# Opening of a two-layer hybrid encoder kernel: x sent ahead of the modulation weights, the last quarter of the modulation formed by ScalarE and GpSimd, and the first five weight tiles split by halves

## What is computed

```python
c_act = jax.nn.silu(c)
for l in range(DEPTH):
    mod = c_act @ w_ada[l] + b_ada[l]                    # w_ada[l]: 1024 x 3072
    shift, scale, gate = jnp.split(mod, 3, axis=-1)
    h = _rmsnorm(x, norm_w) * (1.0 + scale[:, None]) + shift[:, None]
    proj = h @ w_in                                      # 1024 x 8464 columns, split among the mixers
```

## Time and profile before

| | |
|---|---|
| median of three runs | 1181.65 us |
| the profiled execution: time | 1183.2 us |
| the profiled execution: span | 1181.5 us |
| TensorE busy | 1144.8 us, 97% of the span |
| VectorE, ScalarE, GpSimd busy | 629.0, 514.1 and 518.0 us |
| mean granted clock of TensorE | 0.984 |
| moved by DMA | 139.22 MB |

### The profile page before, as it was taken

The page is one execution under the profiler, slowest core; times in us unless marked ns, Lnnn a source line. Parts: engine busy times, 40 slices in busy tenths (PEclk is TensorE's granted clock), DMA queues, the critical chain, the costliest instruction groups (busy, mean ns, idle before and its releaser), DMA issues.

```text
span 1181.5 us, 15202 instructions
## 1 busy us (share of the span) xinstructions
PE 1144.8 (97%) x5890; PEld 940.5 (80%) x5890; DVE 629.0 (53%) x758; ACT 514.1 (44%) x881; POOL 518.0 (44%) x381
## 2 busy tenths in 40 slices
PE   4999999999999999999999999999999999999997
PEld 3778888878888878888887788888788887888886
DVE  5806256558877545436350534565877753232274
ACT  4245355655344533223333634565455553232332
POOL 2334524434343455545524454444343435454541
PEclk9799999999999999999989999999999999999998
DMA  9745522335434445544314472322534423433332
GB/s 304 203 102 164 160 72 74 94 93 140 118 90 107 121 147 161 161 143 125 92 54 116 120 230 72 90 72 90 143 89 107 120 73 85 109 96 107 90 99 81
DMA packets 222200, 139.22 MB, mean 118 GB/s; under 512 B 11912, under 2 KB 212656, under 8 KB 222128
## 3 DMA queue, kind: packets, MB, share of 16 engines
q1 hardware_dynamic: 221480, 137.59, 40.9%
q10 hardware_dynamic: 648, 0.66, 0.2%
HBM read 135.08 MB, written 2.62 MB: 117 GB/s over the span
## 4 chain that ended last, share of the span: by engine, by line
PE 88%; DMA 5%; DVE 3%; POOL 1%; SPq 1%; ACT 1%; issue 1%; DVEq 0%; ACTq 0%
PE main L520 76%; DMA raw<-in_w_in 4%; PE psC L520 3%; PE psA L520 3%; PE psB L520 3%; POOL w_lo L481 1%; DVE xbc L1441 1%; SPq L429 1%; DMA xbc<-in_x 1%; PE psB L683 1%; PE psB L703 0%; ACT w_hi L871 0%; DVE psC L1167 0%; DVE misc L1321 0%; SPq L317 0%
## 5 line engine op out<-in xcount | busy, mean ns | idle before, releaser
L481 POOL TENSOR_TENSOR w_lo<-raw,w_hi 128x512 fp32r<-128x512 f32 x352 | 502.5, 1448 | 629.3 <-ACT w_hi L871 629.1
L520 PE MATMUL main<-h_hi,w_hi 128*128 128x512 f32 x1136 | 454.8, 400 | 10.4 <-POOL w_lo L481 5.5
L520 PE MATMUL main<-h_hi,w_lo 128*128 128x512 f32 x1136 | 445.2, 392 | 0.0
L520 PE MATMUL main<-h_lo,w_hi 128*128 128x512 f32 x1136 | 442.9, 391 | 0.0
L871 ACT ACTIVATE w_hi<-raw 128x512 fp32r<-128x512 f32 x352 | 204.1, 623 | 345.1 <-PE main L520 249.7
L520 PEld LDWEIGHTS main<-h_hi,w_hi 128*128 128x128 f32 x1136 | 214.8, 189 | 67.6 <-issue 20.1
L520 PEld LDWEIGHTS main<-h_hi,w_lo 128*128 128x128 f32 x1136 | 214.7, 189 | 46.0
L520 PEld LDWEIGHTS main<-h_lo,w_hi 128*128 128x128 f32 x1136 | 214.8, 189 | 44.7 <-issue 1.9
L1475 DVE TENSOR_TENSOR tmp<-main,misc 128x512 f32<-128x512 f32 x32 | 22.1, 691 | 174.8 <-PE main L520 171.1
L1321 DVE SCALAR_TENSOR_TENSOR misc<-main,cols,misc 128x511 f32<-128x511 f32 (+2 forms) x96 | 71.9, 749 | 65.6 <-ACT misc L871 62.9
L520 PE MATMUL main<-y_hi,w_hi 128*128 128x512 f32 x256 | 101.3, 396 | 0.0
(11 more groups left out here) (238 smaller groups left out, 1104.5 us busy)
## 6 DMA issues: line engine op xcount, KB each, us to landing
raw<-in_w_in SPq DMA_DIRECT2D x128, 512.0 KB, 3.8
xbc<-in_w_ada SPq DMA_DIRECT2D x16, 512.0 KB, 5.0
zs<-in_w_ada SPq DMA_DIRECT2D x16, 512.0 KB, 4.5
raw<-in_w_pc SPq DMA_DIRECT2D x16, 512.0 KB, 3.7
raw<-in_w_out SPq DMA_DIRECT2D x16, 512.0 KB, 3.7
zs<-in_w_ada SPq DMA_DIRECT2D x16, 256.0 KB, 5.4
big<-in_w_ada SPq DMA_DIRECT2D x16, 256.0 KB, 6.0
tmp<-step_rows SPq DMA_DIRECT2D x8, 512.0 KB, 4.1
```

The source lines that it names most:

```text
L481: nc.gpsimd.tensor_tensor(lo_b[:, cut, :], raw_b[:, cut, :], hi_b[:, cut, :].bitcast(F32), ALU.subtract).then_inc(s_split[b], 2 * BT_ // kt)
L520: return nc.tensor.matmul(o, a, b_, start=start, stop=stop)
```

## The change

- SyncE issues the four parts of x first, then quarter 0. The five first tiles are loaded by halves (four blocks, 256 KB each): all five first halves after quarter 0, all five second halves after quarter 1, each with a semaphore of its own. Tile 5 comes whole at the end, as before.
- VectorE copies x parts 0 and 1 only, ahead of quarter 0; the root is computed after the first two steps of quarter 0, the small rows are copied before its last two. It forms quarters 0, 1 and 2.
- ScalarE loads the square root's table ahead of the squares, and copies x parts 2 and 3. After `h_high` of block 3 it forms the eight products of quarter 3 (slab row block times silu(c)), and GpSimd adds them up: seven additions one after another into `buf_b`. The product k (from 3 on) waits for addition k - 2, since there are two buffers for products.
- GpSimd makes the five first halves' low parts, then the five second halves', then the seven additions, then tile 5.
- TensorE transposes all of x first, then the small rows (into `main[0]` in place of `psC0`), spreads the root, and then works four equal rounds: sums of quarter q, then blocks 2q and 2q + 1 of all five tiles.

The core of the diff (semaphore counts of the split parts, in `part_count` and `wait_raw`, follow the new order and are cut short):

```diff
-        quarter_acc = [buf_d[:, 0:512], buf_d[:, 512:1024]]
+        quarter_acc = [buf_d[:, 0:512], buf_d[:, 512:1024], buf_d[:, 0:512], buf_b]
+        scaled = [buf_x[:, 0:512], buf_x[:, 512:1024]]
...
-            quarter(0)
+            def wide(half):
+                cut = slice(half * BT_, (half + 1) * BT_)
+                for i, (u, b) in enumerate(WIDE):
+                    sp.dma_start(w_bufs(0, u, b)[0][:, cut, :], w_in_t[0, :, cut, i * P:(i + 1) * P]
+                                 ).then_inc(s_rawx[i + 6 * half], 16)
+
             for t in range(PAIRS):
                 sp.dma_start(stage_x[:, t, :], x_t[:, t, :]).then_inc(s_xrow[t], 16)
+            quarter(0)
             wide(0)
+            quarter(1)
             wide(1)
-            quarter(1)
-            wide(2)
-            wide(3)
             quarter(2)
-            wide(4)
             quarter(3)
-            wide(5)
+            sp.dma_start(w_bufs(0, 2, 1)[0], w_in_t[0, :, :, 5 * P:6 * P]).then_inc(s_rawx[5], 16)
...
@@ gpsimd
-                for u in range(U_GA + 1):
+                if l == 0:
+                    for half in range(2):
+                        for u, b in WIDE:
+                            split_half(l, u, b, half)
+                    for k in range(1, KT):
+                        pool.wait_ge(s_prod, k + 1)
+                        if k > 1:
+                            pool.wait_ge(s_padd, k - 1)
+                        nc.gpsimd.tensor_tensor(quarter_acc[3], quarter_acc[3], scaled[k % 2], ALU.add
+                                                ).then_inc(s_padd, 1)
+                    split(l, 2, 1)
+                for u in range(U_GA if l == 0 else 0, U_GA + 1):
...
@@ tensor
-                pe.wait_ge(s_adau, (q + 1) * KT)
+                if q < QUARTERS - 1:
+                    pe.wait_ge(s_adau, (q + 1) * KT)
+                else:
+                    pe.wait_ge(s_padd, KT - 1)
...
-            x_rows(0)
+            for t in range(PAIRS):
+                x_rows(t)
+            pe.wait_ge(s_rows, 16 * N_ROWS)
...
-            quarter_sums(0)
-            for t in range(1, PAIRS):
-                x_rows(t)
-            pe.wait_ge(s_cols, 2)
             spread(psC0, rms, 1)
-            for i in range(2):
-                wide_part(i, 0, 2)
-            pe.wait_ge(s_xc, PAIRS)
-            quarter_sums(1)
-            for i in range(2, 4):
-                wide_part(i, 0, 2)
-            for i in range(4):
-                wide_part(i, 2, 4)
-            quarter_sums(2)
-            wide_part(4, 0, 4)
-            for i in range(4):
-                wide_part(i, 4, 6)
-            quarter_sums(3)
-            wide_part(4, 4, 6)
-            for i in range(5):
-                wide_part(i, 6, 8)
+            for q in range(QUARTERS):
+                quarter_sums(q)
+                if q == 0:
+                    pe.wait_ge(s_cols, 2)
+                    pe.wait_ge(s_xca, 2)
+                for i in range(5):
+                    wide_part(i, 2 * q, 2 * q + 2)
...
@@ scalar
+            f(sm[:, 4, 4:5], eps[:, 0:1], ACT.Sqrt)
             for t in range(PAIRS):
                 x_square(t)
             seed(rms, 1)
-            act.wait_ge(s_xT, PAIRS)
-            f(xT[:, :, SEQ - P:SEQ], psB[:, :].rearrange("p (k n) -> p k n", n=P), ACT.Copy).then_inc(s_xc, 1)
+            for t in range(2, PAIRS):
+                act.wait_ge(s_xT, t + 1)
+                f(xT[:, :, t * P:(t + 1) * P], (psA, psB)[t % 2][:, :].rearrange("p (k n) -> p k n", n=P), ACT.Copy
+                  ).then_inc(s_xca, 1)
...
-            for b in range(2):
-                w_hi_half(0, 0, b, 1)
-            w_hi_part(0, 1, 0)
-            w_hi_part(0, 1, 1)
+            for u, b in WIDE[2:]:
+                w_hi_half(0, u, b, 0)
+            for u, b in WIDE:
+                w_hi_half(0, u, b, 1)
             h_high(0, 2)
             h_high(0, 3)
-            w_hi_part(0, 2, 0)
+            for k in range(KT):
+                act.wait_ge(s_ada[4 + k // 2], 64)
+                if k >= 3:
+                    act.wait_ge(s_padd, k - 2)
+                f(scaled[k % 2] if k else quarter_acc[3], quarter_slab[1][:, k], ACT.Copy, scale=fcol[:, k:k + 1]
+                  ).then_inc(s_prod, 1)
             h_high(0, 4)
...
@@ vector
             dve.wait_ge(s_cact, 1)
-            for k in range(KT):
+            x_copy(0)
+            x_copy(1)
+            for k in range(2):
                 use_quarter(0, k)
-            x_copy(0)
+            inverse_root(rms, s_xsq, PAIRS, 1, sm[:, 4])
+            for k in range(2, 6):
+                use_quarter(0, k)
             dve.wait_ge(s_rT, 1)
...
+            for k in range(6, KT):
+                use_quarter(0, k)
             dve.wait_ge(s_cols, 2)
-            x_copy(1)
-            quarter_mod(0)
-            x_copy(2)
-            inverse_root(rms, s_xsq, PAIRS, 1, sm[:, 4])
             for q in range(QUARTERS):
-                if q > 0:
-                    for k in range(0 if q == 1 else 2, KT):
-                        use_quarter(q, k)
-                    if q < QUARTERS - 1:
-                        for k in range(2):
-                            use_quarter(q + 1, k)
-                    quarter_mod(q)
+                quarter_mod(q)
                 if q == 0:
                     dve.wait_ge(rms[3], 1)
-                    dve.wait_ge(s_xc, PAIRS)
+                    dve.wait_ge(s_xc, 2)
+                    dve.wait_ge(s_xca, 2)
                 h_32(0, 2 * q)
                 h_32(0, 2 * q + 1)
                 h_low(0, 2 * q)
                 h_low(0, 2 * q + 1)
+                if q < 2:
+                    for k in range(KT):
+                        use_quarter(q + 1, k)
```

More of the change, by code:

```diff
@@ L191, in build @@
         s_raw, s_split = sem2("raw_loaded"), sem2("w_split")
-        s_rawx = [sem(f"raw_wide_loaded{i}") for i in range(4)]
+        s_rawx = [sem(f"raw_wide_loaded{i}") for i in range(11)]
         s_hi = sem2("w_hi_done")
@@ L207, in build @@
         s_adau = sem("ada_used")
+        s_prod, s_padd, s_xca = sem("ada_scaled"), sem("ada_added"), sem("x_copied_by_act")
         s_adam, s_mod = sem("ada_summed"), sem("mod_done")
@@ L288, in w_bufs, with part_count, wait_raw @@
             return raw[:, b], w_hi[:, b], w_lo[:, b]
-        def part_count(l, u, half):
+        def part_count(l, u, half, b):
+            if l == 0 and u < U_GA:
+                return u + 1 + (3 - b) * half if (u, b) != (2, 1) else 5 + half
             return (l * COUPLES + u) * 2 + half + 1
-        def wait_raw(eng, l, u, b):
-            if is_wide(l, u):
-                eng.wait_ge(s_rawx[2 * u + b - 2], 16)
+        def wait_raw(eng, l, u, b, half):
+            if l == 0 and u < U_GA:
+                eng.wait_ge(s_rawx[2 * u + b + (6 * half if (u, b) != (2, 1) else 0)], 16)
             else:
-                eng.wait_ge(s_raw[b], (l * COUPLES + u + 1 - (2 if l + u > 0 else 0)) * 16)
+                eng.wait_ge(s_raw[b], (l * COUPLES + u - 2) * 16)
         gate_slab = [xbc[:, 2 * i:2 * i + 2, :].rearrange("p a b -> p (a b)") for i in range(2)]
@@ L436, in next_slab @@
                         if n >= 4:
-                            sp.wait_ge(s_adau, QUARTERS * KT + n - 3)
+                            sp.wait_ge(s_adau, 3 * KT + n - 3)
                         ada_slab(half, k, n)
@@ L479, in split_half @@
                 cut = slice(half * BT_, (half + 1) * BT_)
-                pool.wait_ge(s_hi[b], part_count(l, u, half) if kt == KT else (l * COUPLES + u) * 2 + 2)
+                pool.wait_ge(s_hi[b], part_count(l, u, half, b) if kt == KT else (l * COUPLES + u) * 2 + 2)
                 nc.gpsimd.tensor_tensor(lo_b[:, cut, :], raw_b[:, cut, :], hi_b[:, cut, :].bitcast(F32), ALU.subtract
@@ L541, in out_part @@
                 for k in range(k0, k1):
-                    pe.wait_ge(s_split[b], part_count(l, u, k // BT_))
+                    pe.wait_ge(s_split[b], part_count(l, u, k // BT_, b))
                     pe.wait_ge(s_m, l * KT + k + 1)
@@ L598, in quarter_sums @@
             def quarter_sums(q):
-                pe.wait_ge(s_adau, (q + 1) * KT)
+                if q < QUARTERS - 1:
+                    pe.wait_ge(s_adau, (q + 1) * KT)
+                else:
+                    pe.wait_ge(s_padd, KT - 1)
                 for j in range(QUARTERS):
-                    last = mm(quarter_ps[q][:, q * QUARTERS + j:q * QUARTERS + j + 1], quarter_acc[q % 2][:, j * P:(j + 1) * P],
+                    last = mm(quarter_ps[q][:, q * QUARTERS + j:q * QUARTERS + j + 1], quarter_acc[q][:, j * P:(j + 1) * P],
                               ones[:, 0:1])
@@ L606, in half_sums @@
             def half_sums(half):
-                pe.wait_ge(s_adau, QUARTERS * KT + (half + 1) * KT)
+                pe.wait_ge(s_adau, 3 * KT + (half + 1) * KT)
                 for j in range(KT):
@@ L626, in wide_part @@
                 for k in range(k0, k1):
```

(38 more changed lines are left out.)

12 lines of the change are left out of this document (3 added, 9 removed).

## The result

The changed kernel takes 1188.67 us, the median of seven runs (1185.99 to 1190.34), against 1181.75 us for the kernel before in seven runs (1179.92 to 1184.66). The ratio is 1.0046, interval 1.0034 to 1.0057: slower by 4.0 to 6.7 us (the two medians lie 6.9 us apart, a little more than that interval). The same kernel run again beside later experiments gave 1.0049, interval 1.0030 to 1.0068. The profiled execution took 1189.24 us at a span of 1187.4 us. The ratios leave out one execution of all, one of e3_sums3_early that took 4045.74 us at a granted clock of 1.00, and why it took so long is not known.

A forecast was written before the change was run, and what follows sets the result against it. TensorE, busy 97% of the span, was taken as the bound, with only the opening having time to give. +0.3 us plus 2.5 for one clock fall made +2.8, on 1181.65 giving 1184.4 us; range 1180.0 to 1188.5.

The forecast's parts named there:

- steps 1 and 2: Opening: x first, quarter 0's first pair lands at 11.8 us, first matmul at 25.0 against 26.99, a gain of 2.0.
- Halves (3): Weight loads by halves: five more issues, 3 us of SyncE's queue, cost nothing; up to 3 us without its lead.
- Round 0 (4): First 30 matmuls: 12 at half speed, 18 at full speed, 9.4 us, ending at 34.4.
- Round 1 (5): Second 30 matmuls: at full speed from 38.2 to 45.1 us.
- rival A: Later rounds: each of three stops brings TensorE's clock down, +7.0 us, 1188.6 us; chance 0.15.
- Quarter 3 (6): ScalarE's products and GpSimd's additions: last product ends at 48.0 us and bounds round 2, whose first matmul is at 49.7.
- Round 3 (7): Last round: sums of quarter 3 stand behind all of round 2; first matmul at 60.4, end at 67.3 us.
- the term of the clock: Stops of 2.85 us between rounds: one clock fall in the later rounds, +2.5 us, with none and three as ends.

The follow-up runs named there:

- e3_sums3_early: Changed kernel with the column sums of quarter 3 issued by TensorE after the first tile of round 2 instead of after the last; ratio to the kernel before 1.0021.
- e5: Changed kernel with the five tiles loaded whole after quarter 0 instead of by halves; ratio to the kernel before 1.0045.
- c1: Changed kernel with sums of quarters 1 to 3 issued earlier so rounds overlap, and ScalarE's high parts of blocks 4 and 5 after the sixth product; ratio 0.9986.
- c2: c1 with twelve zero matmuls added behind the sums of quarter 2; ratio to the kernel before 0.9989.
- e1: Changed kernel with 11, 23 and 11 zero-weight matmuls added ahead of rounds 1, 2 and 3; ratio to the kernel before 1.0026.
- e2: Changed kernel with quarter 3 formed by VectorE again, ScalarE's products and GpSimd's additions taken out; ratio to the kernel before 1.0034.

## Why the prediction was right or wrong

**The bound and the start (steps 1 and 2): right, a little pessimistic.** Quarter 0's first pair let VectorE start at 11.09 (11.8 taken), the first `h_32` came at 21.42 (22.4 to 22.6), the first matmul at 23.86 (25.0). The gain at the start is 3.1 us against the earlier trace rows, 2.0 were forecast.

**Halves (3): right.** They cost nothing, and e5 shows nothing that they bring either.

**Round 0 (4): right.** 9.1 us, forecast 9.4. It ran at half speed until 28.67.

**Round 1 (5): wrong in the case taken, right in rival A.** 36.82 to 46.29, 9.5 us; forecast 6.9 with the clock up, 9.4 with it down.

**Quarter 3 (6): right in its mechanism, and it bound round 2 as said.** The products took 0.72 instead of 0.57, the additions came 1.43 apart instead of 1.33 (9.84 us from the first's start to the end of the seventh); the last product ended at 48.44, forecast 48.0 and bounded by 48.6. (By the sum's own terms it is 47.2 + 0.57 = 47.8; 0.2 us of the forecast has no row.) But in this execution `h_32` of block 4 ended at 48.4 too, so with the clock down TensorE's own lateness bound round 2 just as much. What the step missed is the slow `h_low` behind it, 1.1 us on the path.

**Round 3 (7): right.** A full stop stood ahead of it. e3 took it away and got 3.0 to 3.3 us back by the ratios.

**The step that failed** is the term of the clock: "I take one fall in the later rounds, +2.5, and keep none and three as ends." All three stops of 2.9 to 3.9 us brought the clock down, in both profiles of the changed kernel. With three, the forecast's own sum for rival A put the tiles' end at +7.0; it came at +6.7 in the first profile and at +4.6 in the second. That +6.7 is so near to +7.0 is in part luck: the start was 1.1 us earlier than forecast and the late `h_low` cost 1.1 us, and the two cancel. The stops were sized right (2.85 forecast, 2.87 measured) and the rows already held both neighbours: 1.36 idle, held, and 2.47 idle, fallen. What the prediction set against rival A, that the sums run within the stop, did not help: 0.95 us of one-column sums stood ahead of each stop and the clock fell all the same. The runs add that it held after 1.71 and 2.35 us (c1, c2) and fell after every stop of 2.86 us and more. A stop of 2.85 us is nearer to the second, and longer than it, so counting one fall in three was a middle between cases and not the likeliest one. The chance of A at 0.15 was too low. The rule cited there, that groups parted by waits may each begin slow (TensorE: Matmul & The Clock Gate, HAM oscillation — how this bites in real kernels, of the Trainium skill), is what this trace shows, in all four rounds of one opening; e1 and c1 show the cure.

**The chances** for the size of the effect held: within 0.5% was the likeliest, and the ratio, 1.0046, lies near its edge, its interval across it. That the forecast of +2.8 us came as near as it did owes something to the middle value it took: neither profile of the changed kernel shows just one fall in the later rounds.

Where the gain of 3.1 us at the first matmul went: the 120 matmuls of the five tiles took 40.0 us before (26.99 to 66.97) and 49.9 us after (23.86 to 73.71). Before, some 21 of them started 0.43 apart, after some 45; 24 more at 0.2 us each are 4.8 of the 9.9 us. The other 5.1 us are TensorE standing still, since rounds that had run into each other now stood apart: three stops of 2.9, 3.9 and 2.9 us, 9.7 in all, against 3.5 before (0.73, 1.45 and 1.36), less 0.9 us that the column sums now take less. Of these 5.1, 1.1 is the late `h_low`.

What stays open: how the loss divides between idle time and clock in the timed runs. e1 says some 2.5 us for the clock of three rounds, its profile 4.8 against the first profile of the changed kernel and 2.7 against the second. Nor was it measured which of the things that c1 moves brings how much.

## What to carry to other kernels

Where the engine that bounds the kernel waits for a chain (sum, small operations, first block), issue the head of that chain in its queue as soon as its input can be there, and keep some of the old round's work to cover it; "all of round q, then the sums of q + 1" is a full stop each time. Price such a stop twice, as idle time and as the lower clock behind it, and take the neighbouring stop of the trace for whether the clock holds. Work taken off an engine brings nothing if that engine was ahead of the one that asks for its result.

## What the runs showed of the hardware that was not expected

An operation of VectorE that reads two operands from SBUF stood still while GpSimd's tensor_tensor, which also reads two, was running, and went on the moment it ended. In the changed kernel, single instructions of VectorE and GpSimd around 50 us:

```profile
49.22 1.80 DVE L1217 SCALAR_TENSOR_TENSOR h_lo<-tmp,mod,h_hi 128x512 fp32r<-128x512 f32 x1
50.94 1.75 DVE L1217 SCALAR_TENSOR_TENSOR h_lo<-tmp,mod,h_hi 128x512 fp32r<-128x512 f32 x1
...
49.19 1.27 POOL L505 TENSOR_TENSOR tmp<-tmp 128x512 f32<-128x512 f32 x1
50.44 1.70 POOL L484 TENSOR_TENSOR y_lo<-xbc,y_hi 128x512 fp32r<-128x512 f32 x1
```

The addition ends at 50.46 and `h_low`, issued 0.03 us after it, ends 0.56 later at 51.02. The next `h_low` ends at 52.69, 0.55 after GpSimd's operation ended at 52.14; that operation itself took 1.70 instead of some 1.27. In e2, without the additions, and in c1, where GpSimd had nothing to do until the last 0.1 us of them, the same two low parts took 1.42 together. The small operation of c2 is the same case: issued at 32.95, it ended at 34.07, when GpSimd's row below ended at 30.26 + 3.78 = 34.04.

```profile
30.26 3.78 POOL L486 TENSOR_TENSOR y_lo<-xbc,y_hi 128x512 fp32r<-128x512 f32 x3
```

VectorE's steps of the modulation, with one operand in PSUM, kept their 0.857 us beside GpSimd's operations throughout. The Trainium skill (SBUF — State Buffer, SBUF: two separate sides) has this as a lock on a port pair that the two engines share, held for a whole instruction; these rows agree. In an order with little slack, an operation of 0.16 us can therefore take 1.12.
